# Second block's first norm finished on the vector engine and turned by the unit matrix, with reordered output pieces

## The reference

```
def layer_norm(x, g, b):
    mu = jnp.mean(xf, axis=-1, keepdims=True)
    var = jnp.mean(jnp.square(xf - mu), axis=-1, keepdims=True)
    y = (xf - mu) * lax.rsqrt(var + LN_EPS)
    return (y * g + b)
...
mix = token_mixer(x, ...)                       # ends in  y @ w_out   (1024 x 1024)
x = layer_norm(DEEPNORM_ALPHA * x + mix, ln1_g, ln1_b)
ffn = conv_ffn(x, w_up, conv_w, conv_b, w_down) # x @ w_up (1024 x 5632), conv, gelu, @ w_down
x = layer_norm(DEEPNORM_ALPHA * x + ffn, ln2_g, ln2_b)
```

## Time and the profile before

| what | us |
|---|---|
| median of 3 runs | 1187.41 (1185.72 to 1188.49) |
| the profiled execution's own time | 1188.35 |
| its span in the trace | 1186.0 |
| TensorE busy in the span | 1049.0 |
| VectorE busy | 826.8 |
| ScalarE busy | 421.4 |
| mean granted clock of TensorE | 0.96 of 2.4 GHz |

### The profile page before, as it was taken

One profiled execution on the slowest core, in us unless ns is written; L12 is line 12 of the kernel. 1 busy time (PEld: TensorE's weight loads), 2 busy tenths in 40 slices (PEclk: granted clock), 3 DMA queues, 4 the chain that ended last, 5 costly groups with the idle time before them and its releaser, 6 DMA issues.

```text
span 1186.0 us, 13400 instructions
## 1 busy us (share of the span) xinstructions
PE 1049.0 (88%) x4906; PEld 700.6 (59%) x4906; DVE 826.8 (70%) x1909; ACT 421.4 (36%) x879; POOL 296.4 (25%) x262
## 2 busy tenths in 40 slices
PE   5999999999989986876886988777889999999997
PEld 3799976654444542332332333233389979999986
DVE  5699765767677678778887555555566877888843
ACT  3545622313332132222222111111264655665631
POOL 0000001355354542543543544444000000000000
PEclk9999999999999997988988899989989998999999
DMA  9976593999999999999999999999694343554530
GB/s 371 425 324 273 239 403 156 381 392 421 421 421 421 421 421 421 421 422 420 419 421 421 416 422 421 422 421 421 275 375 169 143 178 103 218 212 153 204 142 36
DMA packets 48052, 390.42 MB, mean 329 GB/s; under 512 B 5482, under 2 KB 5874, under 8 KB 7284
## 3 DMA queue, kind: packets, MB, share of 16 engines
q0 software_dynamic: 37040, 269.51, 55.0%
q1 hardware_dynamic: 10948, 120.07, 26.0%
HBM read 388.50 MB, written 1.06 MB: 328 GB/s over the span
## 4 chain that ended last, share of the span: by engine, by line
PE 54%; DMA 30%; DVE 11%; ACT 2%; issue 1%; POOL 1%; SPq 1%; another core or an unknown queue 0%; DVEq 0%; POOLq 0%
DMA ring<-in_uv,idx 25%; PE ps L1429 18%; PE ps L1783 15%; PE ps L1909 5%; DMA ring<-in_w_ada 4%; DVE ring L1229 3%; PE ps L1634 2%; PE ps L1581 2%; PE ps L1839 2%; PE ps L1451 2%; PE ps L1651 1%; POOL ring L490 1%; DVE ring L880 1%; PE ps L1480 1%; PE ps L1491 1%
## 5 line engine op out<-in xcount | busy, mean ns | idle before, releaser
L1783 PE MATMUL ps<-ring,probT 128*128 128x512 f32 x1020 | 492.3, 629 | 103.2 <-ACT probT L743 102.6
L1229 DVE CUSTOM_DVE_ANT_0 ring<-h2t,ring 128x1024 f32<-128x1024 f32 x255 | 308.7, 1222 | 168.5 <-DMA ring<-in_uv,idx 167.9
L1783 PEld LDWEIGHTS ps<-ring,probT 128*128 128x128 f32 x1020 | 199.0, 201 | 347.8 <-issue 201.8
L490 POOL DMA_INDIRECT ring<-in_uv,idx x255 | 293.9, 1153 | 339.6 <-PE ps L1783 279.8
L1429 PE MATMUL ps<-util_r,ring_r 128*128 128x256 f32 x1312 | 218.1, 284 | 1.6 <-DVE util_r L1201 1.6
L1429 PEld LDWEIGHTS ps<-util_r,ring_r 128*128 128x128 f32 x1312 | 183.0, 191 | 3.5 <-DVE ring_r L869 2.7
L869 DVE TENSOR_TENSOR ring_r<-ring,ring_r 128x1024 fp32r<-128x1024 f32 x134 | 157.7, 1221 | 31.1 <-ACT ring_r L512 30.9
L738 ACT ACTIVATE prob<-prob 128x2 f32<-128x2 f32 (+2 forms) x94 | 19.2, 204 | 369.6 <-DVE prob L1229 369.5
L512 ACT ACTIVATE ring_r<-ring 128x1024 fp32r<-128x1024 f32 x134 | 133.9, 1051 | 44.8 <-DMA ring<-in_w_in 21.6
L1429 PE MATMUL ps<-h_r,ring_r 128*128 128x256 f32 x704 | 125.5, 281 | 0.0
L743 ACT ACTIVATE probT<-ct,prob 128x128 f32<-128x128 f32 x256 | 85.1, 392 | 73.8 <-DVE prob L1235 69.9
(11 more groups left out here) (214 smaller groups left out, 968.6 us busy)
## 6 DMA issues: line engine op xcount, KB each, us to landing
ring<-in_w_in SPq DMA_DIRECT2D x13, 2048.0 KB, 12.9
ring<-in_w_up SPq DMA_DIRECT2D x11, 2048.0 KB, 7.8
ring<-in_w_ada SPq DMA_DIRECT2D x7, 2048.0 KB, 9.8
ring<-in_w_down SPq DMA_DIRECT2D x6, 2048.0 KB, 7.8
ring<-in_w_ada SPq DMA_DIRECT2D x8, 1024.0 KB, 15.9
ring<-in_w_out SPq DMA_DIRECT2D x4, 2048.0 KB, 8.0
ring<-in_w_q SPq DMA_DIRECT2D x3, 2048.0 KB, 11.3
ring<-in_w_br SPq DMA_DIRECT2D x2, 2048.0 KB, 12.8
```

The lines of the kernel that those rows point to most:

```text
L490: e.indirect_dma_start(out=row_buf[n], out_offset=None, in_=uv, in_offset=bass.IndirectOffsetOnAxis(ap=idx[:, tt, k:k + 1], axis=0)).then_inc(
L1229: e.tensor_tensor_reduce(u, h2t[:, tt, :], u, 1.0, 0.0, ALU.mult, ALU.add, av[:, tt, n % 128:n % 128 + 1]).then_inc(*made.put(("dot", n)))
L1783: ins = e.matmul(acc[half][:, :], diag[:, n % 8, :], row_buf[n][:, D + half * 512:D + (half + 1) * 512], start=(k == 0), stop=(k == 127))
```

## The change

Both versions compute the same norm. The changed kernel makes all of it on VectorE, before the turn: `row_normed` computes (centred x) * rstd + bias, in two halves, back into `xt`, and TensorE turns the finished x by the unit matrix (`turned_x4`), into fresh PSUM groups. The one-row products, the diagonal matrices of this norm and their scalar are gone. `x4_again` becomes one multiplication by alpha in place, and the bias is no longer multiplied. `row_mean` is split into `row_sum` (for the halves named) and `row_mean`. VectorE sums half 0 of tile 1 between centring tile 0 and `row_normed(0)`, and half 1 after it. ScalarE makes both tiles' squares and roots before its four copies. The low parts are made half by half (both tiles' half 0 first). TensorE's last pieces of the output projection are cut by single k, so that tile 0 is finished earlier; their number is the same.

```
 ScalarE
             sqrt_table(46)
             centred_squares(4, 0)
             row_root(4, 0)
-            turned_high(4, h_r, 0, 0)
             centred_squares(4, 1)
             row_root(4, 1)
-            turned_high(4, h_r, 0, 1)
-            for half in range(2):
-                turned_high(4, h_r, 1, half)
+            for tt in range(2):
+                for half in range(2):
+                    turned_high(4, h_r, tt, half)
 VectorE
+            def row_normed(tt):
+                row_rstd(4, tt)
+                dve.wait_ge(made, ("row rstd", 4, tt))
+                dve.wait_ge(made, ("row gain", 4, tt))
+                for half in range(2):
+                    e.scalar_tensor_tensor(xt[:, tt, HALF[half]], xg[4][:, tt, HALF[half]], col(4, tt, "rstd"),
+                                           ln1[1][:, HALF[half]], ALU.mult, ALU.add).then_inc(
+                        *made.put(("row normed", 4, tt, half)))
             def x4_again(tt):
-                dve.wait_ge(made, ("row rstd alpha", 4, tt))
-                dve.wait_ge(made, "b1 alpha")
-                e.scalar_tensor_tensor(xt[:, tt, :], xg[4][:, tt, :], col(4, tt, "rstd alpha"), ln1[1], ALU.mult,
-                                       ALU.add).then_inc(*made.put(("x4", tt)))
+                dve.wait_ge(done, ("turned x", 4, tt, 1))
+                e.tensor_scalar(xt[:, tt, :], xt[:, tt, :], ALPHA, None, ALU.mult).then_inc(*made.put(("x4", tt)))
...
-            row_mean(4, 0, "mix2", (made, ("x3", 0)))
+            dve.wait_ge(once["b1"], 0)
+            row_sum(4, 0, "mix2", range(2), (made, ("x3", 0)))
+            row_mean(4, 0)
             row_centre(4, 0, ln1[0])
-            row_diagonal(4, 0)
-            row_mean(4, 1, "mix2", (made, ("x3", 1)))
+            row_sum(4, 1, "mix2", (0,), (made, ("x3", 1)))
+            row_normed(0)
+            row_sum(4, 1, "mix2", (1,))
+            row_mean(4, 1)
             row_centre(4, 1, ln1[0])
-            row_diagonal(4, 1)
-            for tt in range(2):
-                for half in range(2):
+            row_normed(1)
+            for half in range(2):
+                for tt in range(2):
                     turned_low(4, h_r, lo_r, tt, half)
-            dve.wait_ge(once["b1"], 0)
-            dve.wait_ge(done, ("shift x", 1))
-            e.tensor_scalar(ln1[1], ln1[1], ALPHA, None, ALU.mult).then_inc(*made.put("b1 alpha"))
             for tt in range(2):
                 x4_again(tt)
 TensorE
+            def turned_x4(tt):
+                for half in range(2):
+                    pe.wait_ge(made, ("row normed", 4, tt, half))
                     o = group(("turned x", 4, tt, half))
                     for k in range(4):
                         c = 512 * half + k * P
+                        ins = e.matmul(o[:, k * P:(k + 1) * P], xt[:, tt, c:c + P], ident, start=True, stop=True)
...
-                if s in (6, 7, 8):
+                if s in (6, 7):
                     for tt in range(2):
-                        out2(s // 8, s % 2, tt, range(2 if s == 8 else 4))
+                        out2(0, s % 2, tt, range(4))
+                if s == 8:
+                    for half in range(2):
+                        out2(1, half, 0, range(2))
...
-                if s == 8:
-                    for tt in range(2):
-                        out2(1, 1, tt, range(2))
+            for half in range(2):
+                out2(1, half, 0, (2,))
+            out2(1, 0, 1, range(2))
+            for half in range(2):
+                out2(1, half, 0, (3,))
+            out2(1, 0, 1, (2, 3))
+            out2(1, 1, 1, range(4))
             for tt in range(2):
-                for half in range(2):
-                    out2(1, half, tt, range(2, 4))
-            for tt in range(2):
-                shift_x(tt)
-            for tt in range(2):
-                turned_x(4, tt)
+                turned_x4(tt)
```

More of the change, by code:

```diff
@@ L979, in row_diagonal @@
                     dve.wait_ge(done, ("turn", 1, 7))
-                if n == 4:
-                    dve.wait_ge(done, ("turn", 2, 15))
                 e.tensor_scalar(by_rstd[tt], ident, col(n, tt, "rstd"), None, ALU.mult).then_inc(
                     *made.put(("row diagonal", n, tt)))
-                if n > 2:
+                if n == 3:
                     e.tensor_scalar(col(n, tt, "rstd alpha"), col(n, tt, "rstd"), ALPHA, None, ALU.mult).then_inc(
@@ L1302, in vector, with row_sum @@
                     head_mask(2 * s + 3)
-            def row_mean(n, tt, name, *ready):
+            def row_sum(n, tt, name, halves, *ready):
                 for event in ready:
                     dve.wait_ge(*event)
-                for half in range(2):
+                for half in halves:
                     dve.wait_ge(done, (name, tt, half))
@@ L1315, in row_mean @@
                         *made.put(("row sum", n, tt, half)))
+            def row_mean(n, tt):
                 dve.wait_ge(made, ("row sum", n, tt, 1))
@@ L1399, in vector @@
             for tt in range(2):
-                row_mean(5, tt, "down", (made, ("x4", tt)))
+                row_sum(5, tt, "down", range(2), (made, ("x4", tt)))
+                row_mean(5, tt)
                 row_centre(5, tt, ln2[0])
@@ L1747, in tensor, with turned_x @@
             second_tile_queries()
-            def shift_x(tt):
-                pe.wait_ge(once["b1"], 0)
+            def turned_x(n, tt):
+                pe.wait_ge(made, ("row diagonal", n, tt))
                 for half in range(2):
+                    pe.wait_ge(made, ("row gain", n, tt, half))
+                    o = group(("turned x", n, tt, half))
+                    for k in range(4):
+                        c = 512 * half + k * P
+                        ins = e.matmul(o[:, k * P:(k + 1) * P], xg[n][:, tt, c:c + P], by_rstd[tt], start=True, stop=True)
+                    ins.then_inc(*done.put(("turned x", n, tt, half)))
+                    banks.give(("turned x", n, tt, half), made, ("x low", n, tt, half))
+            def turned_x4(tt):
+                for half in range(2):
+                    pe.wait_ge(made, ("row normed", 4, tt, half))
                     o = group(("turned x", 4, tt, half))
@@ L1755, in shift_x @@
                         c = 512 * half + k * P
[L1756 to L1772, removed]
+                        ins = e.matmul(o[:, k * P:(k + 1) * P], xt[:, tt, c:c + P], ident, start=True, stop=True)
+                    ins.then_inc(*done.put(("turned x", 4, tt, half)))
+                    banks.give(("turned x", 4, tt, half), made, ("x low", 4, tt, half))
             for n in range(256):
```

## The result

The changed kernel took 1181.34 us in the median of 5 runs (1180.65 to 1183.93), the kernel before 1187.55 (1185.72 to 1188.49). The ratio is 0.9954 with a 95% interval of 0.994 to 0.9968: faster by 0.32 to 0.6%, in the middle 5.5 us. Whether the mechanism held is read from the profiles.

The account below looks back on a forecast made before the run. TensorE alone bounds from w_up's start, which comes 4.31 us earlier; plus 0.27 us of clock makes 4.58, taken as 4.6: 1187.41 - 4.6 = 1182.8 us. Range 1181.4 to 1185.3 us.

Parts of the forecast that it names:

- What bounds the kernel: From w_up's start to the end TensorE alone bounds; each microsecond w_up starts earlier comes off the end, if weights are there.
- The one-row products: Before tile 0's turning: their 3.76 us leave TensorE's path; the clock fell after 3.83 us of them without idle time.
- The pieces: End of output projection: finer pieces let VectorE begin tile 0 at 976.47 instead of 977.17 us, at no cost.
- ScalarE's order: Tile 1's squares stood behind a copy delayed by one-row products; without that copy in front they could start at about 983.3.
- Tile 1 and the join: Tile 1's turning starts at 985.31 instead of 988.71; 2.67 us later w_up starts at 987.98, 4.31 us earlier.
- The last low part: In w_up's start: ready at about 989.05, before its products at about 989.4, so just covered; otherwise costs 0.3 us.
- The clock: Around tile 1's turning: no fall in the 2.16 us gap, saving 0.27 us in w_up; forecast chance 0.52.
- rival 1: Clock falls in the gap before tile 1's turning, costing 1.18 us: gain 3.4, time 1184.0 us; chance 0.33.
- Rival 2: In w_up a wait for weights gives the gain back; taking 3 of the 4.6 us gives 1185.8; chance 0.07.
- Rival 3: Slower: clock falls and stays at 1.2 GHz into w_up, 13.6 us at half giving 1189.6 us; chance 0.04.
- Rival 4: Nothing changes because tile 1 was bound otherwise, on VectorE; no such case seen beyond a weight wait, no chance given.

Follow-up runs that it names:

- 128 rows: Kernel before with both squares ahead of ScalarE's copies, its 32 one-row instructions replaced by ones of 128 rows; ratio 0.9975.
- squares first: Kernel before with ScalarE's order alone changed, both tiles' squares ahead of all copies; ratio 0.9991.
- old pieces: Changed kernel with the old order of the output projection's pieces put back; ratio 0.9967.
- one-row products back: Changed kernel with the 32 one-row instructions put back in front of the turning, their result overwritten; ratio 0.9985.
- filler: Changed kernel with 16 more turning instructions of tile 0, result unread, in TensorE's gap before tile 1; ratios 0.9952 and 0.9965.

## Why the prediction was right, step by step

**What bounds the kernel.** Right. Behind the first w_up product TensorE has no wait in any of the profiles, and what the start gains comes off the end. Where the clock was up from the start, it is 186.8 us to the end of w_down in each (125.2 + 61.6).

**The one-row products.** Right as what costs both, time and clock. Removing them alone gives 4.2 us from B to w_up (19.77 to 15.56). I had read the clock's part off an interval with no idle time before the fall; the pair with one row and 128 rows supports that reading, with one execution each.

**The pieces.** 0.7 us for tile 0's begin was expected, 0.69 measured (4.63 to 3.94 after B). That they matter only together with the new vector order I had not said.

**ScalarE's order.** I named it as what held tile 1, and this was half of it. It held tile 1 because of the one-row products in front of the copy. Without them it is worth 0.2 us, and with them and the clock down nothing (20.01 against 19.75). With 32 products in place and the clock up it would count, by an estimate: in the kernel before tile 1's turning began at 16.17, and 2.66 from there to w_up at full clock (third execution of the changed kernel) give 18.8, where squares first and clock up gave 16.42. Of those 3.3 us between 19.75 and 16.42 the clock alone makes some 0.9, and the order 2.4, which it gives only where the clock stays up. No run has the old order with the clock up, so this split is not shown.

**Tile 1 and the join.** Turning expected 12.77 us after B, measured 12.66 to 12.68; w_up expected 15.44, measured 15.33 where the clock stayed up. Saved until w_up 19.75 - 15.33 = 4.4 us, expected 4.31. The last low part was covered, as expected.

**The clock.** The step with the wrong chance. I took no fall as likelier (0.52 to 0.33); it fell in two of the changed kernel's three profiled executions. Its price was set too high: 0.3 to 0.4 + 0.5, that is 0.8 to 0.9 us, where I had 1.18, since the clock falls not at the gap's end but 0.6 us into tile 1, so that only a part of the turning is slow. That the stage gave the 4.6 us of the forecast in one execution of three, and 3.7 in another, is the luck of the execution; the forecast took the first for the likelier case, and the profiles do not bear that out. From B to the end of w_down the change saves 206.7 - 202.1 = 4.6 us where it stays up (forecast 4.6), and 206.7 - 203.0 = 3.7 where it falls (rival 1: 3.4). The rule of the Trainium skill that I had set against mine ("TensorE: Matmul & The Clock Gate", section "HAM oscillation — how this bites in real kernels": waits between short bursts of matmuls throttle the engine) fits four executions of six, with gaps of 1.8 to 2.1 us. I had stretched it, though: the waits that the section describes are waits for DMA and longer than any of these gaps, so its words did not call for a fall here. The traces decide: short gaps went with a fall in four of six, and the 2.24 us gap that kept the clock, longer than all four, shows again that the length doesn't decide alone.

**The other rivals.** Rival 2: no wait for weights in w_up appeared. Rival 3: the clock was back 1.2 us after w_up's first product at the latest in the changed kernel's profiles; no long stretch at half. Rival 4 did not occur.

**What stays open.** The stage accounts for 3.7 to 4.6 us, a ratio of 0.9961 to 0.9969. The three measured ratios are 0.9954, 0.9958 and 0.9959; each interval holds 0.9961 and up to at least 0.9968, but all three lie on the same side, some 0.3 to 1.8 us beyond. B stood at 972.54 and 969.26 before and at 967.93, 969.02 and 970.61 in the changed kernel, and at 967.03 to 972.20 in all others, changed or not. The five profiles with the work of the kernel before ahead of B have B at 969.2 in the mean, the seven of the changed kernel's variants with new pieces at 969.7, and the one with old pieces at 967.03. So nothing in these profiles shows a gain ahead of B, and with this scatter they are too few to exclude one of a microsecond. That the first measurement came out 1.5 us below my forecast is therefore not explained by a step of it, only not contradicted. Also open is why w_up took 120 ns for a product in one execution (0.36 us for three, at a granted clock of 1.00) and 118.3 to 118.4 in the twelve others; it cost about 1.7 us there, w_down was not touched (61.62 us), and it did not come back in two more executions of the same kernel.

## What to carry to other kernels

A product with one row took TensorE as much time here as a full one, and the clock fell with it in every execution; a bias that another engine can add in a multiplication it makes anyway is better added there. When a list's order seems to hold a chain, ask what makes the instruction ahead of it late: removing that cause was worth 4.2 us, and the order was then worth 0.2. In a kernel whose early stages vary by some microseconds from one execution to the next, read a late stage from a point at its own beginning in both traces, and not from the spans.

## What the runs showed of the hardware that was not expected

At 2.4 GHz, 32 instructions with one row took about as long as 32 with 128 rows (3.76 us in the kernel before against 3.6, from the first to what follows them). But the granted clock fell in all four profiles that have the one-row ones, with TensorE never idle before: among them in two (squares first, one-row products back), at their end in one, and 1.1 us behind them in the first execution of the kernel before (11.3 to 13.5 us after B). It didn't in the one profile where they had 128 rows. There, turning both tiles by full float32 products with the diagonal matrices went at 1.00 for as long as it ran, 3.74 us on end behind 3.73 us of others. In all three executions in which no gap of more than 0.3 us lay ahead of tile 1 and no one-row product stood there (128 rows, filler twice) the clock stayed up; with an open gap it fell in four of six. And in executions of one and the same kernel, with the same gap of 2.05 us in the same place, the clock fell in two and stayed in the third.

The start of the late stage moved by 5.5 us between executions (967.03 to 972.54) whose work ahead of it is the same but for the order of a few products. In the first pair nearly all of the difference of 4.61 us came from the first 48 products of the second block, 2.76 from their later start and 1.80 from a clock that was down in one of the two.
